# One stage's conditioning sums: VectorE adds weight rows, TensorE folds partitions once per unit

## The reference, cut to what matters

```
mod   = split(silu(c)     @ ada_w[i] + ada_b[i], 6)     # ada_w[i]: 1024 x 6144
mod_c = split(silu(c_ctx) @ ada_w[i] + ada_b[i], 6)
h     = LN(x) * (1 + mod[1]) + mod[0]                   # before the mixers
P     = h @ w_in                                        # the input projection
x     = LN(alpha*x + mod[2]*mixers(P)); x = LN(alpha*x + mod[5]*ffn(LN(x)*(1+mod[4]) + mod[3]))
```

## Time and profile before

| | us |
|---|---|
| median of 3 runs | 3681.58 (3672.54 to 3681.80) |
| time of the profiled execution | 3691.22 |
| its span | 3689.3 |
| TensorE busy (matmul) | 3394.2, 92% of the span |
| VectorE busy | 1588.7, 43% |
| ScalarE busy | 1268.4, 34% |
| GpSimd busy | 1074.9, 29% |
| mean granted TensorE clock | 0.968 |

### The profile page before, as it was taken

One profiled execution on the slowest core, in us unless ns is written; L12 is line 12 of the kernel. 1 busy time (PEld: TensorE's weight loads), 2 busy tenths in 40 slices (PEclk: granted clock), 3 DMA queues, 4 the chain that ended last, 5 costly groups with the idle time before them and its releaser, 6 DMA issues. The chain is left out here.

```text
span 3689.3 us, 82751 instructions
## 1 busy us (share of the span) xinstructions
PE 3394.2 (92%) x36725; PEld 2707.4 (73%) x36725; DVE 1588.7 (43%) x2538; ACT 1268.4 (34%) x2184; POOL 1074.9 (29%) x645
## 2 busy tenths in 40 slices
PE   6999999999888999899999899999999888879998
PEld 4668887888655777687878676877778566568887
DVE  3243335442277646612112734445453376372224
ACT  3323233333265422321222243334334365233222
POOL 1111133233011512233333232233333014235453
PEclk9999999999899999899999999999999899989999
DMA  7663332443122333233332145334443223423332
GB/s 265 204 202 112 108 113 87 115 124 91 65 75 76 118 123 124 80 114 119 115 114 96 49 146 173 105 111 122 122 122 93 89 65 120 149 92 109 97 97 86
DMA packets 444285, 423.43 MB, mean 115 GB/s; under 512 B 15588, under 2 KB 371082, under 8 KB 437018
## 3 DMA queue, kind: packets, MB, share of 16 engines
q1 hardware_dynamic: 442346, 409.35, 35.4%
q10 hardware_dynamic: 1584, 8.78, 0.6%
HBM read 329.34 MB, written 88.74 MB: 113 GB/s over the span
## 5 line engine op out<-in xcount | busy, mean ns | idle before, releaser
L886 PE MATMUL ps<-I-322_h_hi,I-325_w_hi 128*128 128x256 f32 (+1 forms) x832 | 298.4, 359 | 4.5 <-PEq L123 4.5
L886 PE MATMUL ps<-I-323_h_lo,I-325_w_hi 128*128 128x256 f32 (+1 forms) x832 | 283.1, 340 | 0.0
L886 PE MATMUL ps<-I-322_h_hi,I-326_w_lo 128*128 128x256 f32 (+1 forms) x832 | 282.3, 339 | 0.0
L2354 POOL TENSOR_TENSOR I-18796_w_lo<-I-18794_w_raw,I-18795_w_hi 128x1024 fp32r<-128x1024 f32 x60 | 144.9, 2416 | 343.5 <-ACT I-18795_w_hi L2317 343.4
L886 PE MATMUL ps<-I-23546_h_hi,I-23549_w_hi 128*128 128x512 f32 (+1 forms) x544 | 214.1, 394 | 4.5 <-PEq L123 4.5
L886 PE MATMUL ps<-I-23547_h_lo,I-23549_w_hi 128*128 128x512 f32 (+1 forms) x544 | 202.5, 372 | 0.0
L886 PE MATMUL ps<-I-23546_h_hi,I-23550_w_lo 128*128 128x512 f32 (+1 forms) x544 | 202.3, 372 | 0.0
L2354 POOL TENSOR_TENSOR I-39027_w_lo<-I-39025_w_raw,I-39026_w_hi 128x1024 fp32r<-128x1024 f32 x60 | 144.4, 2407 | 154.7 <-ACT I-39026_w_hi L2317 154.7
L2317 ACT ACTIVATE I-18795_w_hi<-I-18794_w_raw 128x1024 fp32r<-128x1024 f32 x61 | 64.6, 1059 | 355.6 <-PE ps L364 235.9
L364 PE MATMUL ps<-I-18791_h_hi,I-18795_w_hi 128*128 128x512 f32 x704 | 182.9, 341 | 1.1 <-DVE I-18792_h_lo L401 1.1
L364 PE MATMUL ps<-I-18791_h_hi,I-18796_w_lo 128*128 128x512 f32 x704 | 181.7, 339 | 0.0
(11 more groups left out here) (902 smaller groups left out, 8788.5 us busy)
## 6 DMA issues: line engine op xcount, KB each, us to landing
I-324_w_raw<-in_w_in SPq DMA_DIRECT2D x67, 512.0 KB, 5.7
I-23548_w_raw<-in_w_in SPq DMA_DIRECT2D x67, 512.0 KB, 5.2
I-18804_ada_w<-in_ada_w SPq DMA_DIRECT2D x24, 1024.0 KB, 5.9
I-18794_w_raw<-in_ffn_up SPq DMA_DIRECT2D x44, 512.0 KB, 3.8
I-39025_w_raw<-in_ffn_up SPq DMA_DIRECT2D x44, 512.0 KB, 3.8
proj_d<-I-2000_result SPq DMA_DIRECT2D x52, 384.0 KB, 3.0
I-508_ada_w<-in_ada_w SPq DMA_DIRECT2D x16, 1024.0 KB, 5.8
I-18794_w_raw<-in_ffn_down SPq DMA_DIRECT2D x22, 512.0 KB, 3.4
```

What stands on the lines that cost most here:

```text
L886: m = pe.matmul(bank(6 + i % 2, n_c), w[:, k, :], hv[:, k, c0:c0 + n_c], start=k == 0 and v == 0, stop=k == KT - 1 and v == 2)
L2354: pool.tensor_tensor(pair(g)[1], rings[0][:, g % 3, :, :], pair(g)[0].bitcast(F32), ALU.subtract).then_inc(sem("w_lo"), 1)
```

## The change

In this stage alone the row sums of the modulation go to VectorE. The ring has two slots. For each entry, behind the shifts of tile n, VectorE multiplies the 128 x 2048 weight tile by a column of `cc` and adds it into an accumulator, once for each of the two conditioning vectors (`ada_sums`); the first entry of a unit only multiplies. `ada_used` now counts VectorE's entries. TensorE adds the 128 partitions once per unit with a stationary of ones in one column (`ada_reduce`, eight matmuls), behind tile 8 and at the end of the stage. `pick` and the accumulator are new buffers.

```
-                ring = sb(s2, "ada_w", [P, 3, 2048]) if ada else None
+                ring = sb(s2, "ada_w", [P, 2, 2048]) if ada else None
+                acc = sb(s2, "ada_sums", [P, 2, 2048]) if ada else None
+                pick = sb(s2, "pick", [P, 2, 2]) if ada else None
...
+                    def ada_reduce(u):
+                        pe.wait_ge(sem("ada_used"), KT * (u + 1))
+                        pe.wait_ge(sem("pick"), 3)
+                        for r in range(2):
+                            for q in range(4):
+                                m = pe.matmul(ps[32 * q:32 * q + 2, 6 * 512:7 * 512], pick[:, r, :], acc[:, r, q * 512:(q + 1) * 512],
+                                              start=r == 0, stop=r == 1)
+                        m.then_inc(sem("ada_sum"), 1)
...
                         beside(2 * n + 1)
                         if ada:
-                            ada_step(pe, sem, ring, n, 6)
+                            if n == 8:
+                                ada_reduce(0)
                             if n == 9:
                                 ada_flip(pe, sem, 0, 7)
                     if ada:
-                        ada_step(pe, sem, ring, N, 6)
+                        ada_reduce(1)
                         ada_flip(pe, sem, 1, 7)
                     beside(2 * N)
...
+                    def ada_rows(u):
+                        act.wait_ge(sem("ada_sum"), u + 1)
...
+                    def ada_sums(e):
+                        k, w = ada[e][2], ring[:, e % 2, :]
+                        dve.wait_ge(sem(f"ada_in{e % 2}"), 16 * (e // 2 + 1))
+                        if k == 0 and e:
+                            dve.wait_ge(sem("ada_sum"), 1)
+                        for r, done in enumerate(("ada_first", "ada_used")):
+                            a = acc[:, r, :]
+                            if k == 0:
+                                m = dve.tensor_scalar(a, w, cc[:, k, r:r + 1], None, ALU.mult)
+                            else:
+                                dve.wait_ge(sem(done), e)
+                                m = dve.scalar_tensor_tensor(a, w, cc[:, k, r:r + 1], a, ALU.mult, ALU.add)
+                            m.then_inc(sem(done), 1)
...
+                        if ada:
+                            ada_sums(n)
                         if n == 11 and ada:
                             ada_add(dve, sem, 0, 0, 1, 7)
                         if n == N - 2:
                             normed(0)
+                    if ada:
+                        ada_sums(N)
                     normed(2)
                     normed(3)
```

More of the change, by code:

```diff
@@ L599, in _ @@
                 def _(act):
+                    def ada_rows(u):
+                        act.wait_ge(sem("ada_sum"), u + 1)
+                        if u:
+                            act.wait_ge(sem("ada_T"), u)
+                        for q in range(4):
+                            m = act.activation(ada_row[32 * q:32 * q + 2, :], ps[32 * q:32 * q + 2, 6 * 512:7 * 512], ACT.Copy)
+                        m.then_inc(sem("ada_row"), 1)
                     def beside(p):
@@ L634, in _ @@
                         if ada and n == 8:
-                            ada_copy(act, sem, 0, 6)
+                            ada_rows(0)
                     split_hi(act, sem, rings, N + 1)
                     if ada:
-                        ada_copy(act, sem, 1, 6)
+                        ada_rows(1)
                 @block.gpsimd
@@ L649, in normed @@
                         dve.scalar_tensor_tensor(kk[:, t, :], kf[:, t, :], col("kk", t), side, ALU.mult, ALU.mult).then_inc(sem("kk_done"), 1)
+                    def ada_sums(e):
[12 more added lines that the diff above has]
+                    if ada:
+                        dve.memset(pick[:, :, :], 0.0).then_inc(sem("pick"), 1)
+                        dve.wait_ge(sem("pick"), 1)
+                        for r in range(2):
+                            dve.memset(pick[:, r, r:r + 1], 1.0).then_inc(sem("pick"), 1)
                     for n in range(N):
```

## The result

The changed kernel took 3729.1 us, the median of four runs (3725.6 to 3740.5); the kernel before, run beside it, 3681.7 (3672.5 to 3681.8). The ratio is 1.0144, 95% interval 1.0126 to 1.0161: **47 us slower, 1.4%**. The forecast of 3740 lies 11 above, and its range holds the result.

What follows compares the result with a forecast made beforehand. TensorE was taken to bound the stage, VectorE having some 9 us a tile to spare. Stalls 63.7, clock 13.4 and folds 3.9, less 23.1 saved, gave +58 on 3681.6: 3740 us, range 3716 to 3765.

Steps and rivals of the forecast that it cites:

- the likeliest case: In this stage, waits queued behind the new ones cost more than the removed steps save: +50 to +65, chance 0.79.
- Item 1: Tile 3: its weights, issued behind load 2, are split only after TensorE is ready: +1.5 us.
- Items 2 and 3: Behind tiles 5 and 6: TensorE waits for LORA pieces 4 and 6, held by late LORA stores: +14.0 and +6.9 us.
- Item 4: Tiles 7 to 11 run on TensorE; at tile 12 the weights, again issued late, cost +1.9 us.
- Item 5: Middle of tile 12 and one tile later: LORA stores 4 and 5 delay pieces 12 and 14: +11.2 and +12.0 us.
- Item 6: Middle of tile 14: SPREAD waits for normed(0), which stands behind two sums and a split: +4.2 us.
- Item 7: End of the stage: TensorE idles while VectorE does four sums behind the last shifts: +12.0 us.
- Item 8: Lower TensorE clock: 2.3 us after each of five stalls of 4.2 us or more, 1.9 for the last fold: +13.4.
- A: In the stage VectorE's spare time covers the sums and TensorE loses only its steps: -19 us, 3662; chance 0.02.
- B: The two-slot ring still hides its loads and nothing queued behind is late: +1 us, 3683; chance 0.03.
- C: LORA stores land in time, so the TensorE waits on them shrink to late weights: about +15 us, 3697; chance 0.06.
- D: VectorE's sums are slower beside everything else, 2.9 us each: +72 us, 3754; at twice the price +98, 3780; chance 0.10.

Runs made afterwards that it cites:

- stores first: The change with its two slots, SP starting the modulation's load last in each pass, behind the stores, ahead of the next weights: 3687.3 us, ratio 1.0010.
- three slots: The change with three ring slots in place of two, room made by moving inv into x: 3682.2 us, ratio 0.9997 against the kernel before.
- the version that beats both: The change with three slots, stores and next weights ahead of the modulation's load, normed first, entries 14 and 15 on TensorE: 3632.8 us, ratio 0.9877.
- 48 back: The change with 48 tiny matmuls of two columns ahead of its last fold: 3742.8 us, ratio 1.0178 against the kernel before.
- 8 back: The change with 8 tiny matmuls ahead of its last fold, 40 matmuls fewer than the kernel before: 3719.5 us, ratio 1.0108.

## Why the prediction was right, and where it wasn't

Right was the likeliest case by its mechanism, at all its places and near its sizes, although the result, 3729.1, lies 2 us below that case's own range (3731 to 3748). By its items:

- **Item 1** (tile 3, +1.5): a wait of 1.48 for GpSimd. **Items 2 and 3** (+14.0, +6.9): 11.85 and 7.23. Item 2 is the larger miss: LORA store 0 landed at 123.65, where 125.3 was forecast.
- **Item 4** (+1.9): 1.08 and 0.57 for the weights of tiles 11 and 12. In addition a wait of 2.76 behind tile 11 that I hadn't listed: ACT's split of the late weights stands ahead of that LORA piece.
- **Item 5** (+11.2, +12.0): 10.56 and 12.78. **Item 6** (+4.2): 3.91. **Item 7** (+12.0): 11.81.
- Together 64.0 us of new waits against 63.7. Which queue they come from is shown by the variants: stores first takes away 46.6 of the stage's 62.2, three slots 51.5.
- **Item 8** (clock, +13.4) was too small. The granted clock in the stretches behind five of the waits, until it was back, and in the last fold:

```profile
124.97:131.00 6.03, 6.03 (x21) 4.70 (x22) 5.26 (x6) 3.24 (x5) 2.72 (x1) 0.57 0.00 0
145.16:151.00 5.84, 5.84 (x19) 4.54 (x20) 5.07 (x6) 3.23 (x5) 2.53 (x1) 0.53 0.00 0
225.40:231.40 6.00, 6.00 (x25) 4.70 (x26) 0.00 (x0) 1.73 (x3) 2.37 (x1) 0.68 0.01 3
250.46:257.00 6.54, 6.54 (x22) 5.12 (x23) 0.00 (x0) 1.73 (x3) 2.37 (x1) 0.54 0.42 116
268.12:279.60 11.48, 11.48 (x32) 7.70 (x32) 1.51 (x2) 1.43 (x2) 0.00 (x0) 0.61 0.84 292
291.42:294.60 3.18, 3.17 (x16) 0.40 (x16) 0.87 (x1) 0.00 (x0) 0.00 (x0) 0.59 0.31 124
```

Length times one minus the clock gives 2.6, 2.7, 1.9, 3.0, 4.5 and 1.3, 16.0 in all, and 1.7 more behind the wait of 2.76 (5.75 us at 0.70). With 17.7 in place of 13.4 the sum is 64.0 + 17.7 + 3.9 - 23.1 = 62.5, and measured are 62.2. The term of 2.3 a wait fitted a wait of 4.8 us; behind the wait of 3.91, which came soon after that of 12.78, the clock stayed at its lower level, 1.2 GHz, for some 9 us.

- **The sum on VectorE**, 2.27 us, was between the shortest and the middle one (2.24 and 2.34), the multiply-only one 1.3 (1.29), and the exclusion with GpSimd is there: a pair with a split between takes 6.74, the 4.60 of a pair and nearly a split more. It struck four pairs of twelve in full and one in part (5.69), and not most tiles as forecast.
- **"Outside the stage nothing changes" is the step that failed.** The scan stage became 11.6 us shorter (744.6 to 733.0). Without that the span would have grown by 61, and the time would have stood at about 3741; with TensorE's program as long as before the change did measure 3742.8. So the 11 us between forecast and result are mostly the position of TensorE's code: in the profiles the stage is 4 us above its forecast, the scan stage 12 below, the rest of the span 1 below, and the medians differ by 2 us less than the profiles. That the first two have opposite signs is luck; without the 4 in the stage, the forecast would have been 15 off. The step lacked a question that the trace of before could have raised, what the waits named "issue" in the scan stage hang from.
- **Rivals.** A (-19, 3662): false in this order of queues; in the version that beats both, which has other edits besides, the stage is 18.1 shorter, near its price, so what failed was its condition. B (the short ring still hides its loads): false, two slots cost the kernel before 20 us in the stage. C (LORA stores in time, +15): false for the change; the version that starts the stores first has its figure in the stage, +15.6. D (slower sums): false, 2.34.

## What to carry to other kernels

Where an edit adds a wait to an in-order queue, list what stands behind it: here the store behind the load that waited held up ACT and through it TensorE for 45 us. Moving the waiting item to the end of its pass, or one more slot, took most of it back. Work given to an idle engine must leave the last critical step ahead of itself, and its own last entries may go where they were done before. And before a difference of 1% is put down to an edit, look at a stage that wasn't edited: if its waits named "issue" differ, pad the program to its old length and measure again.

## What the runs showed of the hardware that I had not expected

**The time of a stretch depends on where its instructions stand in TensorE's program.** 24 matmuls more make the scan stage 21 us shorter, 40 fewer 22 to 24, 48 fewer 10 to 14. In the kernel before the longer of these waits come in pairs, one in a burst of small products and one in the next burst. The first pair, in the order of time of weight loads and of matmuls:

```profile
268.26 0.56 PEld L909 LDWEIGHTS ps<-I-1982_Bh,I-1992_kk_in 64*64 64x64 f32 x32
268.72 0.56 PEld L909 LDWEIGHTS ps<-I-1992_kk_in,I-1978_EN 64*64 64x64 f32 x32
...
270.14 0.20 PEld L909 LDWEIGHTS ps<-I-1992_kk_in,I-1982_Bh 64*64 64x64 f32 x4
271.37 0.54 PEld L909 LDWEIGHTS ps<-I-1992_kk_in,I-1982_Bh 64*64 64x64 f32 x28 [1.03 <-issue]
```

```profile
285.16 0.56 PE L909 MATMUL ps<-I-1993_kk_in,I-1983_Bh 64*64 64x64 f32 x19 [2.00 <-issue]
```

The trace has 254 weight loads from the one to the other. In each of the five pairs that follow it has 254 or 255, and from each pair to the next 2030 or 2031, eight times as many. The row of the DMA queues that carries instructions reads, for the scan stage of the kernel before:

```profile
q8 instruction: 109, 1.79, 1.0%
```

That is 16.4 KB a packet. The Trainium skill, page "Perfetto Trace Analysis", section "The 4-stage abstract model", says that an instruction has 64 bytes. By that figure the 13829 matmuls and 13830 weight loads of the stage are an estimated 1.77 MB, which agrees with the row, a packet holds an estimated 256 of them, and 254 weight loads with their matmuls are two packets.

Each packet has a record of its own in the trace, with start and duration. All twelve waits at L909 end 1.26 to 1.52 us after a 16 KB packet of this queue has ended, and the twelve of the run with 48 back 1.25 to 1.60 us after. For the wait that ends at 285.16 the packet ran from 282.82 to 283.80. For the longest, which ends at 401.32, it ran from 398.53 to 399.80, and TensorE had been idle since 398.18, so it stood still before the packet's record began.

The same number accounts for 24 more and 40 fewer doing the same. Each of the matmuls that these edits add or leave out stands in the trace as two matmuls with two weight loads, four instructions (36629 in place of 36725 matmuls with 48 fewer). So 24 more and 40 fewer are 64 matmuls or 256 instructions apart, by the estimate one packet. And the few waits that the one has left come back in the other; the run with 8 back (40 fewer) against the 5.0 us in 13 waits of above:

```profile
PEld ps L955 <- issue: 4.9, 13, 0.9
```

So TensorE's program arrives in pieces of 16 KB, and some 20 us of the stage's length hang from where the limits of the pieces fall in its code. The position is shown by the runs, the link to the packets by these times and by the period. Only inferred is the last step: that a piece that is due within a burst (32 weight loads in 0.46 us, 268.26 to 268.72) comes late, while one that is due among the large products is hidden. What starts a packet, and what happens in the 1.3 to 1.6 us behind it, no run shows.

**Four matmuls in four partition groups took the time of one:** 0.97 and 0.95 us a step of 512 columns, float32; two steps in a row, at the end of the stage, took 1.90 and 1.88. The Trainium skill, page "TensorEngine Tiling (Array Packing)", section "Key Properties", says that different tiles can work in parallel; the trace agrees. It also means that the sixteen steps that the change removes were already cheap.
